# Expert row lists summed from one-hot products on chip instead of read back from HBM, in a decoder-step kernel

## The chip, the cores and the metric

The kernel runs on one core of one Trainium2 chip. The metric is the device time of one launch in microseconds, the median of several runs. The profile is one execution of the same program taken by the hardware profiler; its times count from the start of its span.

## What is computed

One layer of a hybrid decoder over 512 prompt tokens and 8 x 4 sample tokens (544 rows of width 1024, all float32). A token-mixing half (a gated delta rule beside a forgetting attention) is followed by the channel-mixing half, where the change lies:

```python
def _moe(h, w_router, router_bias, w_gate, w_up, w_down, ws_gate, ws_up, ws_down):
    s = jax.nn.sigmoid((x @ w_router).astype(jnp.float32))
    sb = s + router_bias.astype(jnp.float32)
    grp = sb.reshape(n_tok, N_GROUPS, N_EXPERTS // N_GROUPS)
    gscore = jnp.sum(lax.top_k(grp, 2)[0], axis=-1)
    _, gidx = lax.top_k(gscore, TOPK_GROUPS)
    ...
    _, eidx = lax.top_k(jnp.where(emask, sb, -jnp.inf), TOP_K)
    ...
    def expert(acc, xs):
        wg, wu, wd, ge = xs
        y = (jax.nn.silu(x @ wg) * (x @ wu)) @ wd
        return acc + ge[:, None] * y.astype(jnp.float32), None
    ...
    shared = (jax.nn.silu(x @ ws_gate) * (x @ ws_up)) @ ws_down
```

Each token goes to 8 of 64 experts (inner width 256), and all tokens to one shared expert of the same width.

## The kernel before

The program is a series of phases. The last one, from about 715 us on, holds the output projection, the layer norm, the router, the shared expert, the routed experts and the final sum. Tokens lie in five tiles: 0 to 3 of 128 rows, tile 4 of the 32 sample rows.
The router's part, per tile t: TensorE transposes the normed rows (`h2_transposes`) and makes the `logits`; ScalarE takes the sigmoid; VectorE picks eight experts (`choose`, 22 short instructions in a chain); TensorE counts, by a product with a triangular matrix, how many earlier tokens chose each expert (`place`); VectorE makes from it the address 768 x expert + place of each of the token's eight entries (`address`). POOL then writes the token's entry numbers to these addresses of a list in HBM, one indirect DMA for each of the eight columns (`enter` on POOL, 34 in all). After the last tile `totals`, `counts`, `rank_experts` and `sort` order the experts by the number of their tokens. The order goes to HBM (`order_row`), where SP reads it to load expert weights by rank (`load_by_rank`).

The routed experts run as 46 units, a list fixed when the program is built. A unit serves 128 rows of one expert, or of two whose lists are short. POOL reads the lists back in rank order (`ranked`, one gather), VectorE doubles and quadruples their heads (`twice`, `quad`), TensorE transposes them (`unit_rows`), and VectorE makes row numbers of them for the gathers and scatters of all units (`unit_indices`).

Then comes the loop over units. TensorE, unit u: transposes of unit u-1's hidden rows (`hiddenT`), transposes of unit u+1's tokens (`xT`), gate/up product of u (`gate_up_of`), down product of u-1 (`down_of`). Weights sit in a ring of four gate/up slots and five down slots, 3 MB an expert; the load of expert n waits for the last unit that used its slot. POOL gathers tokens three units ahead and scatters each unit's rows.

The shared expert fills gaps: `up(t)` ahead of the loop between the router's products, then `shared_hidden`, `down(t)`, `shared_fold`. Before the change `down` of tiles 0, 1, 2 stands ahead of the loop and those of tiles 3 and 4 stand in it as `shared_step`s (`SHARED_BESIDE`).

## Time and profile before

| what | value |
| --- | --- |
| median of 3 runs | 1521.06 us |
| lowest, highest | 1520.38, 1523.2 us |
| profiled execution, its time | 1513.65 us |
| its span | 1511.8 us |
| mean granted clock of TensorE | 0.964 |
| TensorE (PE) busy | 1383.9 us, 92% |
| VectorE (DVE) busy | 562.8 us, 37% |
| ScalarE (ACT) busy | 291.6 us, 19% |
| GpSimd (POOL) busy | 316.0 us, 21% |
| moved by DMA | 358.50 MB |

Busy time counts an engine's own work, not its waits. A granted clock of 1.00 is full speed. DMA share is the mean busy share of the core's 16 DMA engines.

### The profile page before, as it was taken

Reading aid. Unit: us, or ns where it says so; the run is one execution under the profiler, and the core shown is the slowest. Engines: PE = TensorE matmul, PEld = TensorE weight load, DVE = VectorE, ACT = ScalarE, POOL = GpSimd, SP = SyncE. Lnnn points to the kernel's source line nnn. Section 1 sums busy time; section 2 is a strip of 40 time slices with the busy share of each in tenths; the row PEclk is TensorE's granted clock in tenths of the full one; section 3 lists DMA queues with packets and bytes.
Section 4 is the critical chain, followed back from the end, with each engine's and each line's share of the span. In section 5 each row is a group of like instructions: output and inputs, shape, how many; then the busy total and the mean of one; then the engine's idle time right before and its main releaser. Section 6 shows DMA issues by size and latency. Waiting matters only on the chain. (4 is left out here: it accounts for less than half of the span.)

```text
span 1511.8 us, 21981 instructions
## 1 busy us (share of the span) xinstructions
PE 1383.9 (92%) x8512; PEld 790.9 (52%) x8512; DVE 562.8 (37%) x1292; ACT 291.6 (19%) x674; POOL 316.0 (21%) x334
## 2 busy tenths in 40 slices
PE   5999999999969999899998799998999999999966
PEld 3776777764657776776454334443344333434322
DVE  1101455453633654445886243211111111111138
ACT  1002233453223222111111011111011111101021
POOL 6000000000069994000054111111112111111100
PEclk9999999999989999989999899999999999999988
DMA  9510410123464443685006789999999999999585
GB/s 338 173 56 8 143 58 1 56 85 112 135 185 138 140 138 94 216 289 185 29 29 180 265 362 396 408 415 417 420 401 401 412 419 389 416 412 420 204 315 226
DMA packets 106804, 358.50 MB, mean 237 GB/s; under 512 B 28837, under 2 KB 31013, under 8 KB 80581
## 3 DMA queue, kind: packets, MB, share of 16 engines
q1 hardware_dynamic: 81288, 301.98, 52.0%
q0 software_dynamic: 15968, 40.61, 7.3%
q10 hardware_dynamic: 9446, 14.51, 2.8%
q8 instruction: 68, 1.11, 0.3%
q14 instruction: 34, 0.28, 0.1%
HBM read 331.49 MB, written 38.15 MB: 245 GB/s over the span
## 5 line engine op out<-in xcount | busy, mean ns | idle before, releaser
L2134 PE MATMUL bank<-arena 128*32 128x512 f32 (+2 forms) x1536 | 335.1, 618 | 19.6 <-DMA arena<-in_w_up 17.7
L2134 PEld LDWEIGHTS bank<-arena 128*32 128x32 f32 (+2 forms) x1536 | 121.1, 138 | 201.3 <-issue 198.5
L2142 PE MATMUL bank<-arena 128*32 128x512 f32 (+2 forms) x768 | 168.6, 598 | 0.7 <-DVE arena L2915 0.7
L2121 POOL DMA_INDIRECT expert_rows<-arena x46 | 46.4, 1008 | 485.4 <-PE bank L2127 418.6
L2909 DVE TENSOR_TENSOR arena<-arena,bank 128x256 f32<-128x256 f32 x46 | 19.4, 421 | 320.7 <-ACT arena L2556 320.7
L1210 PE MATMUL bank<-arena 128*128 128x272 f32 x512 | 128.7, 404 | 1.9 <-ACT arena L1247 1.6
L438 PE MATMUL bank<-arena 128*128 128x272 f32 x480 | 113.8, 400 | 2.8 <-PEq L132 1.9
L2142 PEld LDWEIGHTS bank<-arena 128*32 128x32 f32 (+2 forms) x768 | 55.0, 134 | 110.3 <-issue 109.4
L1210 PEld LDWEIGHTS bank<-arena 128*128 128x128 f32 x512 | 95.8, 193 | 28.0 <-issue 7.1
L438 PEld LDWEIGHTS bank<-arena 128*128 128x128 f32 x480 | 92.9, 194 | 23.1 <-issue 2.8
L668 PE MATMUL bank<-arena 128*128 128x272 f32 x384 | 100.3, 405 | 0.0
L455 PE MATMUL bank<-arena 128*128 128x512 f32 (+3 forms) x320 | 91.9, 448 | 0.5 <-DVE arena L2691 0.5
L2556 ACT ACTIVATE arena<-bank 128x256 f32<-128x256 f32 x46 | 17.7, 384 | 344.3 <-PE bank L2134 344.3
L2921 DVE COPY arena<-bank 128x512 f32<-128x512 f32 x46 | 31.8, 692 | 126.9 <-PE bank L2142 126.9
L668 PEld LDWEIGHTS bank<-arena 128*128 128x128 f32 x384 | 70.4, 193 | 13.9 <-issue 1.5
L455 PEld LDWEIGHTS bank<-arena 128*128 128x128 f32 (+1 forms) x320 | 50.3, 199 | 40.8 <-issue 38.6
L2618 POOL DMA_INDIRECT expert_lists<-arena x34 | 38.0, 1117 | 128.1 <-DVE arena L2749 118.7
L2562 ACT COPY arena<-bank 128x512 f32<-128x512 f32 x46 | 27.0, 587 | 152.4 <-PE bank L2142 152.4
L2117 POOL DMA_INDIRECT arena<-h_rows,arena x46 | 46.3, 1007 | 35.1 <-issue 20.8
L1727 POOL MEMSET arena<- 64x128 f32 x2 | 0.4, 198 | 253.1 <-POOLq L1252 253.0
L2127 PE MATMUL bank<-arena 128*128 128x128 f32 x368 | 48.6, 276 | 4.7 <-DVE arena L2771 3.6
L2127 PEld LDWEIGHTS bank<-arena 128*128 128x128 f32 x368 | 42.6, 143 | 5.8 <-DVE arena L2771 3.9
(485 smaller groups left out, 1788.9 us busy)
## 6 DMA issues: line engine op xcount, KB each, us to landing
arena<-in_w_gate SPq DMA_DIRECT2D x64, 1024.0 KB
arena<-in_w_up SPq DMA_DIRECT2D x64, 1024.0 KB
arena<-in_w_down SPq DMA_DIRECT2D x64, 1024.0 KB, 15.3
arena<-in_w_ada SPq DMA_DIRECT2D x12, 2048.0 KB, 9.4
arena<-in_w_in SPq DMA_DIRECT2D x11, 2048.0 KB, 9.9
arena<-expert_rows SPq DMA_DIRECT2D x8, 2048.0 KB, 25.5
gate_logits<-arena ACTq DMA_DIRECT2D x16, 272.0 KB, 3.8
arena<-gate_logits SPq DMA_DIRECT2D x8, 544.0 KB, 5.0
```

The costliest lines, as they stand in the source:

```text
L438: mm = nc.tensor.matmul(pair[i][:, 0:HALF], w[:, k, m * P:(m + 1) * P], rhs[:, k, i * HALF:(i + 1) * HALF], start=k == 0, stop=k == kt - 1)
L455: mm = nc.tensor.matmul(out, lhs[:, k, t * P:t * P + n], w[:, k, cols], start=k == 0, stop=k == kt - 1)
L668: mm = nc.tensor.matmul(out[:, 0:HALF], w[:, k, (m % 4) * P:(m % 4 + 1) * P], hT[:, k, half * HALF:(half + 1) * HALF], start=k == 0, stop= ...
L1210: mm = nc.tensor.matmul(out[:, 0:HALF], w[:, k, m * P:(m + 1) * P], hT[:, k, half * HALF:(half + 1) * HALF], start=k == 0, stop=k == KD - 1)
L2117: return nc.gpsimd.indirect_dma_start(out=into, out_offset=None, in_=h2_d, in_offset=bass.IndirectOffsetOnAxis(ap=rows, axis=0), bounds_ch ...
L2121: return nc.gpsimd.indirect_dma_start(out=y_d, out_offset=bass.IndirectOffsetOnAxis(ap=rows, axis=0), in_=of, in_offset=None, bounds_check ...
L2127: mm = nc.tensor.transpose(bank[half][:, k * P:(k + 1) * P], of[:, kk * P:(kk + 1) * P], ident)
L2134: mm = nc.tensor.matmul(out[rows].rearrange("p (a n) -> p a n", a=2), x[:, k, rows], gate_up_slot(n)[:, :, k, :], start=k == 0, stop=k == ...
L2142: mm = nc.tensor.matmul(out[rows, :], h[:, k, rows], down_slot(n)[:, k, 512 * half:512 * half + 512], start=k == 0, stop=k == 1)
L2562: nc.scalar.copy(Yb[u % RY][:, 0:512], bank[5][:, :]).then_inc(y_a.sem, 1)
L2618: scat.inc(nc.gpsimd.indirect_dma_start(out=list_rows, out_offset=bass.IndirectOffsetOnAxis(ap=adi[:, t, k:k + 1], axis=0), in_=tokval[:, ...
L2921: nc.vector.tensor_copy(Yb[u % RY][:, 512:D], bank[6][:, :]).then_inc(y_v.sem, 1)
```

## The change

The list entries of a tile become two sets of one-hot rows: `ent_e` marks, for each of the eight columns, the token's expert (64 wide, scaled by the entry's number less a constant), and `ent_p` marks the place in that expert's list (192 wide). TensorE multiplies them and sums over all columns and tiles in one PSUM bank (`enter` on TensorE, 34 products), which leaves the first 192 places of every list on chip. One-hot rows are made on POOL for tiles 0, 1, 2 and on VectorE for tiles 3 and 4. `unit_rows` becomes four products with the sorting one-hot `hot`, so that it sorts and transposes at once. POOL still scatters the entries to HBM, where only overflow beyond the fixed units is read: tile 0 as before, tiles 1 to 4 after the first three token gathers. `down` of tile 2 moves into the loop, so that three tiles stand there (`BESIDE`), with another order in each unit. The order of TensorE's list around `enter` is new, VectorE's behind `order_and_excess` too. The load of the first `w_down` waits for the last list product, because one of the `ent_p` tiles lies in its slot.

```diff
@@ -2042,6 +2044,8 @@
         for name, dst, tick in (("w_gate", both[:, 0], gu), ("w_up", both[:, 1], gu), ("w_down", down_slot(n), dn)):
             if name == "w_gate" and n >= RG:
                 sp.wait_ge(gu_mm.sem, LAST_UNIT[n - RG] + 1)
+            if name == "w_down" and dn is dl[0] and n == 0:
+                sp.wait_ge(list_mm.sem, 2 * PT + 1)
             if name == "w_down" and n >= RD:
                 sp.wait_ge(d_mm.sem, LAST_UNIT[n - RD] + 1)
...
 
             def unit_rows():
                 pe.wait_ge(dup_done.sem, 1)
-                nc.tensor.transpose(bank[5][:, 0:E], ranked[:, 0:P], ident[0:E, 0:E])
-                nc.tensor.transpose(bank[5][:, E:2 * E], twice.rearrange("p a n -> p (a n)"), ident[0:E, 0:E])
-                nc.tensor.transpose(bank[5][:, 2 * E:3 * E], ranked[:, P:2 * P], ident[0:E, 0:E])
-                unit_mm.inc(nc.tensor.transpose(bank[5][:, 3 * E:4 * E], quad.rearrange("p a n -> p (a n)"), ident[0:E, 0:E]))
+                nc.tensor.matmul(bank[7][:, 0:E], lists[:, 0:P], hot, start=True, stop=True)
+                nc.tensor.matmul(bank[7][:, E:2 * E], twice.rearrange("p a n -> p (a n)"), hot, start=True, stop=True)
+                nc.tensor.matmul(bank[7][0:ROWS - P, 2 * E:3 * E], lists[:, P:ROWS], hot, start=True, stop=True)
+                unit_mm.inc(nc.tensor.matmul(bank[7][:, 3 * E:4 * E], quad.rearrange("p a n -> p (a n)"), hot, start=True, stop=True))
+
...
+                n = 4 if t < PT else 2
+                pe.wait_ge(ent_made.sem, 2 * t + half + 1) if t < 3 else pe.wait_ge(ent_late.sem, 2 * t + half - 5)
+                for k in range(n):
+                    mm = nc.tensor.matmul(bank[7][E * (k % 2):E * (k % 2) + E, 0:ROWS], ent_e[:, 4 * half + k, :], ent_p[half][:, k, :],
+                                          start=t == 0 and half == 0 and k < 2, stop=t == PT and k >= n - 2)
+                list_mm.inc(mm)
 
             for depth in (range(KD - 1), range(KD - 1, KD)):
                 if depth[0]:
...
@@ -2332,30 +2348,39 @@
                 if t < 2:
                     place(t)
             h2_transposes(3)
-            up(0, 0, 1)
+            up(0, 0, 3)
             place(2)
             logits(3)
-            up(0, 1, KD)
+            up(0, 3, KD)
             h2_transposes(4)
             up(1, 0, 1)
+            enter(0, 0)
+            enter(0, 1)
             logits(4)
-            up(1, 1, 3)
+            up(1, 1, 4)
             place(3)
-            up(1, 3, 6)
+            enter(1, 0)
+            enter(1, 1)
+            up(1, 4, 6)
             place(4)
             up(1, 6, KD)
             counts()
             up(2, 0, 2)
             sort()
-            up(2, 2, KD)
+            enter(2, 0)
+            enter(2, 1)
+            up(2, 2, 5)
             overflow_sums()
-            down(0)
+            enter(3, 0)
+            enter(3, 1)
+            enter(4, 0)
+            up(2, 5, KD)
+            unit_rows()
             up(3)
             table()
             up(4)
-            unit_rows()
+            down(0)
             down(1)
-            down(2)
 
             def shared_step(kind, t):
 
...
-            pe.wait_ge(s_fold.sem, 3)
+            pe.wait_ge(s_fold.sem, 1)
             for u in range(NU):
                 if u:
                     hiddenT(u - 1)
                 if u + 1 < NU:
                     xT(u + 1)
+                if 1 <= u <= len(BESIDE):
+                    shared_step("high", BESIDE[u - 1])
                 gate_up_of(u)
-                if u in SHARED_BESIDE:
-                    shared_step(*SHARED_BESIDE[u][0])
+                if u < len(BESIDE):
+                    shared_step("hiddenT", BESIDE[u])
                 if u:
                     down_of(u - 1)
-                if u in SHARED_BESIDE:
-                    shared_step(*SHARED_BESIDE[u][1])
+                if u < len(BESIDE):
+                    shared_step("low", BESIDE[u])
             hiddenT(NU - 1)
             down_of(NU - 1)
             pe.wait_ge(y_a.sem, NU)
...
-            pool.wait_ge(side_store.sem, 16)
-            for t in range(NT):
+            step = chained(pool, gch)
+            TT, TS = nc.gpsimd.tensor_tensor, nc.gpsimd.tensor_scalar
+
+            def enter_tile(t):
                 pool.wait_ge(addr_done.sem, t + 1)
                 for k in range(TOPK if t < PT else 2):
                     enter(t, k)
-            pool.wait_ge(order_done.sem, 2)
-            pool.wait_ge(x1_done.sem, NT)
-            pool.wait_ge(scat.sem, scat.n)
-            lists_in.inc(nc.gpsimd.indirect_dma_start(out=ranked, out_offset=None, in_=list_d,
-                                                      in_offset=bass.IndirectOffsetOnAxis(ap=order_i.bitcast(U32), axis=0)), 16)
+
+            def one_hots(t):
+                pool.wait_ge(addr_done.sem, t + 1)
+                if t:
+                    pool.wait_ge(list_mm.sem, 2 * t)
+                step(TS(expert_of, a8[:, t, :], 1.0 / LC, -0.5 - 0.5 / LC, ALU.mult, ALU.add))
+                step(TS(expert_of, expert_of, 12582912.0, None, ALU.add))
+                step(TS(expert_of, expert_of, 12582912.0, None, ALU.subtract))
+                step(TS(expert_of, expert_of, float(LC), None, ALU.mult))
+                step(TT(place_of, a8[:, t, :], expert_of, ALU.subtract))
+                for k in range(TOPK):
+                    step(TS(ent_e[:, k, :], key[:, t, :], a8[:, t, k:k + 1], short_val[:, t, k:k + 1], ALU.is_equal, ALU.mult))
+                for k in range(TOPK):
+                    ins = TS(ent_p[k // 4][:, k % 4, :], place1, place_of[:, k:k + 1], None, ALU.is_equal)
+                    ent_made.inc(ins) if k % 4 == 3 else step(ins)
+
+            step(pool.iota(place1, pattern=[[1, ROWS]], base=1, channel_multiplier=0, allow_small_or_imprecise_dtypes=True))
+            pool.wait_ge(tokval_made.sem, 3)
+            step(TS(short_val, tokval, -float(FILL), None, ALU.add))
+            pool.wait_ge(side_store.sem, 16)
+            enter_tile(0)
+            pool.wait_ge(wo_mm.sem, 2 * NT)
+            one_hots(0)
+            one_hots(1)
+            one_hots(2)
...
@@ -2645,6 +2690,8 @@
             pool.wait_ge(su_mm.sem, NT)
             for u in range(RX - 1):
                 gather(u)
+            for t in range(1, NT):
+                enter_tile(t)
             for u in range(NU):
                 if u + RX - 1 < NU:
...
@@ -2750,8 +2797,9 @@
                 else:
                     for q in range(4):
                         rows = slice(QUAD * q, QUAD * q + QUAD)
-                        ins = TS(adi[rows, t, 0:2], a8[rows, t, 2 * q:2 * q + 2], -1.0, None, ALU.add)
-                        done(addr_done, ins) if q == 3 else vch.inc(ins)
+                        ins = nc.vector.tensor_copy(a8s[rows], a8[rows, t, 2 * q:2 * q + 2])
+                        step(ins) if q == 3 else vch.inc(ins)
+                    done(addr_done, TS(adi[:, t, 0:2], a8s, -1.0, None, ALU.add))
...
+            def one_hots(t):
+                n = TOPK if t < PT else 2
+                found, where, to = (a8[:, t, :] if t < PT else a8s), place_of[:, 0:n], expert_of[:, 0:n]
+                over_e, over_p = [P, n, E], [P, min(n, 4), ROWS]
+                dve.wait_ge(list_mm.sem, 2 * t)
+                step(TS(to, found, 1.0 / LC, -0.5 - 0.5 / LC, ALU.mult, ALU.add))
+                step(TS(to, to, 12582912.0, None, ALU.add))
+                step(TS(to, to, 12582912.0, None, ALU.subtract))
+                step(STT(where, to, -float(LC), found, ALU.mult, ALU.add))
+                step(TT(ent_e[:, 0:n], key[:, t, :].unsqueeze(1).to_broadcast(over_e), found.unsqueeze(2).to_broadcast(over_e), ALU.is_equal))
+                step(TT(ent_e[:, 0:n], ent_e[:, 0:n], short_val[:, t, 0:n].unsqueeze(2).to_broadcast(over_e), ALU.mult))
+                for half in range(max(1, n // 4)):
+                    here = where[:, 4 * half:4 * half + min(n, 4)].unsqueeze(2).to_broadcast(over_p)
+                    done(ent_late, TT(ent_p[half][:, 0:min(n, 4)], place1.unsqueeze(1).to_broadcast(over_p), here, ALU.is_equal))
+
+            def lists_out():
+                dve.wait_ge(list_mm.sem, 2 * PT + 1)
+                step(nc.vector.tensor_copy(lists, bank[7][:, 0:ROWS]))
+                step(nc.vector.tensor_copy(quad, bank[7][:, 0:QUAD].unsqueeze(1).to_broadcast([P, 4, QUAD])))
+                done(dup_done, nc.vector.tensor_copy(twice, bank[7][:, 0:64].unsqueeze(1).to_broadcast([P, 2, 64])))
+
...
+                for rows, a, b, c in ((slice(0, P), 0, WIDE, 0), (last, THREE, WIDE, 3 * E + SMALL), (low, WIDE, PAIRED, 2 * E),
+                                      (high, WIDE, PAIRED, E + WIDE), (low, PAIRED, NU, E + PAIRED), (high, PAIRED, NU, E + PAIRED + 6)):
+                    step(TS(units_f[rows, a:b], got[rows, c:c + b - a], float(FILL), None, ALU.add))
                 done(unit_done, row_indices(step, units_f, floor_f, to_rows, from_rows))
...
@@ -2874,23 +2936,24 @@
             totals()
             rank_experts()
             order_and_excess()
+            one_hots(3)
+            one_hots(4)
             shared_hidden(0)
             shared_hidden(1)
+            lists_out()
+            overflow_rows()
+            unit_indices()
+            shared_hidden(2)
             residual(3)
+            overflow_table()
             residual(4)
-            shared_hidden(2)
-            overflow_rows()
+            shared_hidden(3)
+            shared_hidden(4)
             shared_fold(0)
-            shared_hidden(3)
-            overflow_table()
-            shared_hidden(4)
-            unit_indices()
...
+            xT_high(0)
             shared_fold(1)
-            xT_high(0)
-            shared_fold(2)
             for u in range(NU):
                 if u:
                     hiddenT(u - 1)
                 if u + 1 < NU:
                     xT_high(u + 1)
+                if 1 <= u <= len(BESIDE):
+                    fold_beside(1, BESIDE[u - 1])
                 hidden(u)
-                if u in SHARED_BESIDE:
-                    fold_beside(*SHARED_BESIDE[u][0])
                 if u:
                     y_high(u - 1)
-                if u in SHARED_BESIDE:
-                    fold_beside(*SHARED_BESIDE[u][1])
+                if u < len(BESIDE):
+                    fold_beside(0, BESIDE[u])
```

## Rows read from the trace of the kernel before

**Rows 1.** Table of stretches: from:to, length, busy us (instructions) by engine, clock, DMA share, GB/s.
```profile
777.40:857.00 79.60, 63.25 (x224) 32.65 (x222) 47.05 (x163) 10.86 (x20) 33.79 (x32) 0.87 0.62 210
...
869.90:883.90 14.00, 14.00 (x81) 5.28 (x81) 4.51 (x9) 1.51 (x5) 0.00 (x0) 1.00 0.79 317
...
957.00:1441.00 484.00, 459.31 (x2301) 190.32 (x2299) 82.02 (x154) 59.66 (x115) 75.42 (x75) 0.98 0.96 391
```

**Rows 2.** Timeline of PE, 794 to 899 us: start, us, line, shapes, count, idle before.
```profile
794.74 0.68 PE L2228 MATMUL bank<-arena 32*128 32x32 f32 x8 [0.91 <-DVE arena L2707]
...
796.33 2.00 PE L455 MATMUL bank<-arena 128*128 128x64 f32 x16
...
803.05 0.43 PE L2244 MATMUL bank<-arena 32*128 32x64 f32 x2
...
818.46 6.10 PE L2288 MATMUL bank<-arena 128*128 128x512 f32 x8 [3.81 <-ACT arena L2514]
824.39 7.03 PE L2262 MATMUL bank<-arena 128*128 128x512 f32 x16
...
831.51 3.65 PE L2260 MATMUL bank<-arena 128*32 128x256 f32 x32
836.54 0.27 PE L2311 MATMUL bank<-arena 64*128 64x64 f32 x1 [1.39 <-DVE arena L2839]
...
839.55 5.37 PE L2288 MATMUL bank<-arena 128*128 128x512 f32 x8 [2.12 <-DVE arena L2061]
...
845.60 3.70 PE L2288 MATMUL bank<-arena 128*128 128x512 f32 x8 [0.46 <-ACT arena L2514]
...
856.98 8.98 PE L2134 MATMUL bank<-arena 128*32 128x512 f32 x64
...
898.50 1.04 PE L2127 MATMUL bank<-arena 128*128 128x128 f32 x8
```

**Rows 3.** Timeline of POOL, 814 to 841 us.
```profile
814.27 0.95 POOL L2618 DMA_INDIRECT expert_lists<-arena  x1 [0.30 <-issue]
815.53 0.96 POOL L2618 DMA_INDIRECT expert_lists<-arena  x1 [0.30 <-issue]
824.98 0.95 POOL L2628 DMA_INDIRECT arena<-expert_lists,arena  x1 [8.49 <-DMA expert_lists<-arena]
840.27 1.04 POOL L2117 DMA_INDIRECT arena<-h_rows,arena  x1 [14.34 <-DVE arena L2061]
```

**Rows 4.** Timeline of DVE, of choose, the order's copy, the last of unit_indices.
```profile
766.42 0.41 DVE L2739 TENSOR_SCALAR arena<-arena 128x64 f32<-128x64 f32 x1
...
808.45 0.21 DVE L2791 CAST arena<-bank 1x64 int32<-1x64 f32 x1 [0.59 <-PE bank L2297]
...
839.21 0.19 DVE L2061 CAST arena<-arena 128x46 uint32<-128x46 f32 x1
```

**Rows 5.** Table of stretches, while POOL scatters entries and little else moves.
```profile
786.00:792.00 6.00, 6.00 (x13) 2.68 (x13) 5.12 (x9) 1.71 (x3) 4.78 (x5) 0.73 0.02 0
```

**Rows 6.** The page's costliest groups: busy us, mean ns, then idle before.
```profile
L438 PE MATMUL bank<-arena 128*128 128x272 f32 x480 | 113.8, 400 | 2.8 <-PEq L132 1.9
```

**Rows 7.** Groups of POOL by form: busy us, mean ns, then idle before.
```profile
L1766 POOL TENSOR_SCALAR arena<-arena 128x2048 f32<-128x2048 f32 x4 | 21.8, 5442 | 0.4
...
L1762 POOL TENSOR_SCALAR arena<-arena 128x32 f32<-128x32 f32 x4 | 1.5, 367 | 0.4
...
L1746 POOL COPY arena<-arena 64x128 f32<-64x128 f32 x2 | 0.6, 288 | 2.5 <-DMA arena<-sample_gates 2.5
...
L1770 POOL COPY arena<-arena 128x32 f32<-128x32 f32 x1 | 0.2, 210 | 0.1
```

**Rows 8.** Timelines of DVE, POOL and DVE again, earlier in the kernel.
```profile
501.27 2.53 DVE L1553 TENSOR_TENSOR arena<-arena 128x256 f32<-128x256 f32 x1
...
501.18 2.35 POOL L1756 TENSOR_TENSOR arena<-arena 128x1024 f32<-128x1024 f32 x1
...
623.59 0.43 DVE L1553 TENSOR_TENSOR arena<-arena 128x256 f32<-128x256 f32 x1
```

More of the change, by code:

```diff
@@ L1878, in build @@
     gsc, rank8, v8 = (scratch(NT, 8) for i in range(3))
-    adi, base = scratch(NT, 8, dt=U32), scratch(E)
+    base = scratch(E)
     m1s, m2s, ent = scratch(OVER, p=E), scratch(OVER, p=E), scratch(2, p=E)
-    nsort, keyp, rank = scratch(2, p=E), scratch(1, p=E), scratch(1, p=E)
+    nsort, keyp, rank = scratch(2, p=E), scratch(1), scratch(1)
     by_rank, excess, over, sums = scratch(2, p=E), scratch(1, p=E), scratch(1, p=E), scratch(2, p=E)
-    order_i = scratch(1, p=E, dt=I32)
     tab_f, tab_i, count_i = scratch(2, p=OVER), scratch(2, p=OVER, dt=I32), scratch(1, p=E, dt=I32)
-    keyf, cmp_, hot = (at(X0 + 15616 + E * i, E, p=E) for i in range(3))
+    keyf, cmp_, hot = (at(X0 + 15616 + E * i, E) for i in range(3))
     h2_d = nc.dram_tensor("h2_rows", (TOK, D), F32).ap()
@@ L2061, in row_indices @@
         return nc.vector.tensor_copy(to_rows, slots_f)
-    ranked = at(X0 + 12800, LC, p=E)
-    twice, quad = at(X0 + 13568, 2, 64, p=E), at(X0 + 13696, 4, QUAD, p=E)
+    twice, quad, lists = at(X0 + 13568, 2, 64), at(X0 + 13696, 4, QUAD), at(X0 + 13824, ROWS)
+    ent_e, ent_p = at(T2 + 1024, TOPK, E), (at(T1 + 1024, 4, ROWS), at(DN_SLOT[0], 4, ROWS))
+    place1 = at(T1 + 1024 + 4 * ROWS, ROWS)
+    short_val, place_of = at(T1 + 1024 + 5 * ROWS, NT, TOPK), at(T1 + 1064 + 5 * ROWS, TOPK)
+    expert_of, a8s = at(T1 + 1072 + 5 * ROWS, TOPK), at(T1 + 1080 + 5 * ROWS, 2)
+    assert T1 + 1082 + 5 * ROWS <= T1 + 2048 and DN_SLOT[0] + 4 * ROWS <= T1 + 6912 and T2 + 1536 <= WS0
     units_f, floor_f = at(T2, NU), at(T2 + NU, NU)
@@ L2298, in sort @@
-                sort_mm.inc(nc.tensor.matmul(bank[7][0:E, 260:262], hot, nsort, start=True, stop=True))
+                sort_mm.inc(nc.tensor.matmul(bank[4][0:1, 320:384], nsort[:, 0:1], hot[0:E], start=True, stop=True))
+                sort_mm.inc(nc.tensor.matmul(bank[5][0:E, 260:262], hot[0:E], nsort, start=True, stop=True))
             def overflow_sums():
                 pe.wait_ge(over_done.sem, 1)
-                nc.tensor.matmul(bank[7][0:E, 264:265], cumU[0:E, 0:E], over, start=True, stop=True)
@@ L2303, in overflow_sums @@
-                cum_mm.inc(nc.tensor.matmul(bank[7][0:E, 265:266], ones[0:E, 0:E], over, start=True, stop=True))
+                nc.tensor.matmul(bank[5][0:E, 264:265], cumU[0:E, 0:E], over, start=True, stop=True)
+                cum_mm.inc(nc.tensor.matmul(bank[5][0:E, 265:266], ones[0:E, 0:E], over, start=True, stop=True))
             def table():
                 pe.wait_ge(row_done.sem, 1)
-                tab_mm.inc(nc.tensor.matmul(bank[7][0:OVER, 268:270], m1s, ent, start=True, stop=True))
+                tab_mm.inc(nc.tensor.matmul(bank[5][0:OVER, 268:270], m1s, ent, start=True, stop=True))
@@ L2512, in shared_hiddenT @@
                     act.wait_ge(sd_mm.sem, t)
-                src = bank[4 if t < 3 else 7]
+                src = bank[4 if t < 2 else 7]
                 sT_sb.inc(nc.scalar.copy(shT[:, :, 0:n], src[:, 0:2 * n].rearrange("p (k n) -> p k n", k=2)))
@@ L2839, in unit_indices @@
-                done(dup_done, nc.vector.tensor_copy(twice, ranked[:, 0:64].unsqueeze(1).to_broadcast([E, 2, 64])))
                 dve.wait_ge(unit_mm.sem, 1)
-                got = bank[5]
+                got = bank[7]
                 low, high, last = slice(0, 64), slice(64, P), slice(96, P)
-                step(nc.vector.tensor_copy(units_f[:, 0:WIDE], got[:, 0:WIDE]))
-                step(nc.vector.tensor_copy(units_f[last, THREE:WIDE], got[last, 3 * E + SMALL:4 * E]))
-                step(nc.vector.tensor_copy(units_f[low, WIDE:PAIRED], got[low, 2 * E:2 * E + HEAVY]))
```

71 lines of the change are left out of this document (31 added, 40 removed).

## The prediction, made before the changed kernel was run

> **What bounds the kernel now.** I read the page's slices first (where TensorE has holes), then the timelines of the four engines between 763 and 857 us, which is where the diff works, then the table of stretches for the loop over the 46 units behind it. The chain that ended last reaches back only to 1438 us, so it says nothing of this stage.
>
> The loop is closed from both sides [rows 1]: in its second unit, from 869.9 to 883.9 us, TensorE is busy all the time with DMA at 0.79, and from 957 to 1441 us TensorE is busy 459 of 484 us with DMA at 0.96. The reader should see that the loop can't be compressed: it ends a fixed time after it begins. So I ask when the first gate/up product can run. Before, that is at 857.0 us [rows 2].
>
> What leads up to it is a relay. The router's choices become list entries, which POOL scatters to HBM with 34 indirect DMAs, the last at 815.5 us; it waits 8.5 us for them to land, reads the lists back at 825.0 us [rows 3], and the row numbers are ready at 839.4 us [rows 4]. Beside that relay TensorE is not idle: from 777.4 to 857 us it is busy 63.25 of 79.6 us [rows 1]. Only the holes, 16.35 us, can be won there, and of those that the timeline names (0.9, 3.8, 1.4 and 2.1 us [rows 2]) the read-back of the lists explains the last two.
>
> **The change, part by part.**
>
> *Removed.* The wait of 8.5 us, the gather of the lists (825.0 to about 834 us) and one of three shared down products ahead of the loop. Gain on the path: at most the holes above and the product's 0.4 + 3.7 us [rows 2].
>
> *Moved.* 26 of the 34 scatters now stand behind the first three token gathers: 26 x 1.26 us [rows 3] = 33 us of POOL, in front of the gather for unit 3 and the scatter of unit 0. Before, the gathers begin at 840.3 and unit 3's rows are transposed at 898.5 [rows 2, 3], 58 us later; behind the change that gather is issued some 37 us after the first and lands about 10 us later, as the first did (840.3 to 850.4). Hidden by about 11 us; if that cover went, unit 3 would be late. The scatters themselves keep the DMA engines 2% busy [rows 5], 26 of them under 1 us.
>
> *Added on TensorE.* 34 one-hot products with 192 columns. Nearest row: 272 columns, 113.8 us for 480 instructions, 0.237 us each [rows 6]; two instructions are one f32 product, so 192/272 x 0.47 = 0.335 us, and 34 of them 11.4 us. Bounds: 8.5 us (64 columns, 2.00 us for eight products [rows 2]) and 16.1 us (as 272 columns).
>
> *Added on POOL, for tiles 0, 1 and 2.* Each tile is a chain of 21 elementwise instructions, each waiting for the last: 5 of 8 columns, 8 of 64, 8 of 192. The trace has `TENSOR_SCALAR` with a per-partition scalar at 32 columns, 0.366 us, and at 2048 columns, 5.44 us [rows 7], so 2.5 ns a column upon 0.28 us: 0.445 us at 64 and 0.77 us at 192 columns. With 0.25 us for a small one and gaps of 0.085 us: 1.2 + 3.6 + 6.1 + 1.8 = 12.7 us a tile, 9.3 us until its first half is ready. Lower bound from the copy rows, 0.21 us at 32 and 0.29 us at 128 columns [rows 7]: about 7.6 us a tile. I take 12.7, since it is the same operation.
>
> The Trainium skill ("GPSIMD Engine Reference", 4.1 Engine selection) calls one-input elementwise work on GpSimd roughly line-rate; the `TENSOR_SCALAR` row disagrees, the copy rows nearly agree. By that rule a tile would cost about the lower bound and the sum below would be that of the rival "quick POOL".
>
> *What VectorE pays.* With POOL busy, VectorE's two-operand instruction on 256 columns took 2.53 us; it ended at 503.80, 0.27 us behind the POOL instruction that had begun just before it. The same line with POOL idle takes 0.43 [rows 8]. `choose` has 10 instructions of the exposed kinds (7 two-operand ones in SBUF, 3 `TENSOR_SCALAR`; the second kind I count by the 0.41 us that L2739 once took instead of 0.19 [rows 4]). Each waits for what is left of a POOL instruction, about 0.4 us: +4 us a `choose`. POOL waits for them in turn: about +3 us a tile.
>
> The Trainium skill ("SBUF — State Buffer", Who interferes with whom) says the same of these two engines: whichever issues first holds the shared pair for its whole instruction.
>
> *The relay, step by step.* Serialization is the point: `one_hots(t)` on POOL waits until the products of tile t-1 are done, and TensorE meets `enter(t)` in its fixed order, with `place`, `counts` and `sort` queued behind.
> - POOL's tile 0 starts when out_rows(4) is done, 777.5, and ends near 795 (12.7 + 4.5 for VectorE's holds).
> - `choose(2)` +4, the layer norm of tile 4 a little: its h2 is ready at 799.4 instead of 794.7.
> - TensorE: transposes 0.7, up(1,0,1) 1.0, `enter(0)` 2.7: done 803.8.
> - POOL's tile 1: 803.9 + 12.7 + 3.5 = 820.1; `enter(1)` done 821.4. Meanwhile TensorE has only logits(4) 2.0, up 3.0, place(3) 0.6 to do: it stands from 809.4 to 815.5 and again 3 us.
> - up 2.0, `place(4)`: 824, against 803.05 before. Then address(4), totals, counts, ranks, sort: 5.6 us before (803.05 [rows 2] to 808.66 [rows 4]), 8.8 with POOL's tile 2 beside it: the sorted order at 832.6, 24 us later, and with it the first expert weights.
> - POOL's tile 2: 821.5 + 12.7 + 3.8 = 838; `enter(2)` done 839.3.
> - VectorE's tile 3: four small ones 0.8, two of 512 columns and two of 768, which from 0.43 us at 256 [rows 8] are at most 0.86 and 1.3 each; with 0.7 and 1.0, since part of the 0.43 is fixed, 4.2 us: 843.5. `enter(3)` 845.4, tile 4 and its entries 848.0, up(2,5,8) 3.0 beside `lists_out`, `unit_rows` 852.5.
> - up(3) 7.0, up(4) 3.7 (as before [rows 2]): 863.3; POOL's gathers wait for it too: 863.4 instead of 840.3.
> - down(0), down(1) 5.3 each: 873.9; two sets of transposes, first gate/up product 876.5.
>
> So the loop begins 19.5 us later. SP is held as well: `w_down` of load 0 waits for the last list product (848), loads 1 and 2 queue behind it, and 7 MB from 848 at about 400 GB/s are there by 866, before 876.5: no cost, as long as TensorE is that late. In the loop stand 4.1 us more of shared products (a third tile), in units 0 to 3, where TensorE has no hole but DMA has some left (0.79 [rows 1]): I count 2 us of them. Behind the loop nothing changes.
>
> **Sum.** 19.5 + 2 = 21.5 us. The profiled execution took 1513.65 us (span 1511.8), so 1535 for the like; the runs' median is 1521.06, 7.4 us above it, and with the same shift I get 1542.5; I give 1541, since not every exposed instruction will meet POOL in mid-flight.
>
> **Rivals.**
> - *POOL slow, but no blocking of VectorE.* Same relay with 12.7 us a tile and nothing else: h2 of tile 4 at 794.7, `enter(0)` 799.1, tile 1 811.9, `place(4)` 815.7, order 820.7, tile 2 826, `unit_rows` 840.5, gathers 851.3, first product 864.3: +7.3 + 2 = +9.5: 1530. Against it: the 2.53 us.
> - *Quick POOL*, 7.6 us a tile, with blocking: `enter(1)` 812.9, tile 2 822.5, `unit_rows` 838.2, gathers 849, first product 862: +5 + 2 = +7: 1528.
> - *Products ready in time (faster).* If a tile on POOL took under about 5 us, each `enter` would find its one-hots made. Then up(4) ends at 835.2 - 4.1 (holes) - 6.6 (down(0) moved behind) + 11.4 + 1.5 = 837.4; gathers land about 848; down(0), down(1) fill the gap; first product 851.2, 5.8 us earlier, of which the third tile in the loop takes back about 2: -4, 1517. It decides only below 5 us; the cheapest rows give 7.6.
> - *No net change*: the same with half of that eaten by colder clock or the late SP queue: 1521.
> - *Late scatters bite*: if POOL's issue in the loop were slowed by a third or more, unit 3 waits: up to +8 upon the forecast, 1550.
>
> **How the numbers follow.** Forecast 0.50, no blocking 0.18, quick POOL 0.12, late scatters 0.05, faster 0.07, same 0.08. A measurement of this kernel can tell about 0.2%, 3 us. Faster 0.07, same 0.08, slower 0.85. The forecast's own range, from the bounds of the products (-3, +5) and of blocking, is 1534 to 1549; leaving out faster, most of same and the top gives 1524 to 1550.
>
> **What would show it.** Right: POOL's 128x192 instructions at 0.7 us or more; TensorE waiting on POOL ahead of `enter(1)` and `enter(2)` for 15 us together; the store of the sorted order some 20 us later; the first token gather near 863. Wrong: those instructions near 0.35 us, `choose(2)` still 3.9 us long, or a first gate/up product before 857. A wrong slope at 192 columns moves all of it: each 0.1 us there is 0.8 us a tile.

## The result, and the profile of the changed kernel

The changed kernel takes 1560.59 us (median; 1553.21 to 1563.27), the kernel before, run beside it on the same chip, 1522.88: ratio 1.0227, interval 1.019 to 1.0264. It is slower by about 2.3%. The prediction had the direction, but at 1541 us, with a range that ended at 1550, it was too low.

The profiled execution took 1553.21 us (span 1551.1), 39.3 us more of span than the one of before. The first view is TensorE's timeline, the part that answers to [rows 2]: start, us, line, shapes, count, idle before and what ended it.

```profile
791.40 1.06 PE L2237 MATMUL bank<-arena 32*128 32x32 f32 x8 [5.37 <-DVE arena L2754]
...
797.16 2.54 PE L456 MATMUL bank<-arena 128*128 128x64 f32 x16
...
808.00 1.55 PE L2328 MATMUL bank<-arena 128*64 128x192 f32 x8 [5.29 <-POOL arena L2663]
811.32 1.54 PE L2328 MATMUL bank<-arena 128*64 128x192 f32 x8 [1.76 <-POOL arena L2663]
...
815.98 0.43 PE L2253 MATMUL bank<-arena 32*128 32x64 f32 x2
...
826.88 1.55 PE L2328 MATMUL bank<-arena 128*64 128x192 f32 x8 [2.44 <-POOL arena L2663]
...
837.18 0.55 PE L2328 MATMUL bank<-arena 128*64 128x192 f32 x4 [2.19 <-DVE arena L2896]
...
867.82 5.55 PE L2142 MATMUL bank<-arena 128*32 128x512 f32 x39
...
875.92 1.61 PE L2142 MATMUL bank<-arena 128*32 128x512 f32 x2 [1.49 <-issue]
...
880.87 1.01 PE L2142 MATMUL bank<-arena 128*32 128x512 f32 x1 [0.40 <-issue]
...
894.20 1.87 PE L2142 MATMUL bank<-arena 128*32 128x512 f32 x2 [1.79 <-issue]
```

Two things are to be seen. In the upper half the relay of the prediction is there: TensorE waits for GpSimd's one-hots ahead of the list products, and `place(4)`, the line of 2 with 32x64, comes late. In the lower half is something that no step of the prediction has. Unit 0's gate/up product starts at 867.82, and after 39 matmul instructions TensorE begins them one or two at a time. The product is over at 898.7, 30.8 us after its start; before, it took 9.0 [rows 2]. The engine waits for nothing that the profile names ("issue").

The second view is the table of stretches, with the columns of [rows 1]: the stretch from the first late entry DMA until the slow part begins, the slow part, the second unit, and the loop.

```profile
857.20:872.40 15.20, 10.94 (x60) 4.83 (x63) 6.42 (x10) 1.37 (x3) 11.83 (x12) 0.89 0.82 328
872.40:897.00 24.60, 14.59 (x27) 1.93 (x19) 0.00 (x0) 0.00 (x0) 15.66 (x16) 0.59 0.13 35
904.97:921.30 16.33, 15.92 (x85) 6.22 (x85) 5.55 (x13) 1.93 (x4) 2.33 (x2) 1.00 0.74 286
957.00:1441.00 484.00, 461.03 (x2314) 192.40 (x2312) 90.36 (x206) 60.40 (x116) 77.88 (x77) 0.98 1.00 410
```

In 24.6 us TensorE begins 27 matmul instructions, while VectorE and ScalarE begin none and the DMA engines are at 0.13. The granted clock is 0.59 there, but it isn't the cause: a matmul takes 1 us at it, and each group of one or two starts 1.4 to 2.8 us behind the last, with an idle gap between. GpSimd is the one engine that works, and its timeline says on what (it answers to [rows 3]; the last lines of two groups of one-hots stand ahead).

```profile
783.12 10.59 POOL L2663 TENSOR_SCALAR arena<-arena 128x192 f32<-128x192 f32 x8
...
798.98 5.54 POOL L2661 TENSOR_SCALAR arena<-arena 128x64 f32<-128x64 f32 x8
804.62 6.64 POOL L2663 TENSOR_SCALAR arena<-arena 128x192 f32<-128x192 f32 x8
...
853.12 1.14 POOL L2125 DMA_INDIRECT arena<-h_rows,arena  x1 [26.30 <-PE bank L2269]
...
857.18 1.03 POOL L2641 DMA_INDIRECT expert_lists<-arena  x1 [0.30 <-issue]
...
889.29 0.97 POOL L2641 DMA_INDIRECT expert_lists<-arena  x1 [0.30 <-issue]
890.57 1.05 POOL L2125 DMA_INDIRECT arena<-h_rows,arena  x1 [0.30 <-issue]
891.92 1.01 POOL L2125 DMA_INDIRECT arena<-h_rows,arena  x1 [0.30 <-issue]
```

The 26 late entry DMAs and the two gathers behind them run from 857.2 to 892.9. TensorE is back at full pace at 896.3.

**Where the 39.3 us are.** From TensorE's marks in both traces: start of the stage to the transposes of tile 4, -3.3 (791.40 against 794.74); from there to the first gate/up product, +14.2 (76.42 against 62.24); unit 0's product, +21.9; the rest of the way to unit 1, +2.4; units 1 to 3, +2.8; the loop behind that, +1.8; behind the loop, -0.4 (39.4 by rounding). The gate/up products of units 3 and 4 start at 937.42 and 949.07, against 899.47 and 911.13.

**How good the trace of before is.** There is one, and its execution was 7.4 us quicker than the median. The kernels of experiments 2, 5 and 6 below run the instructions of before up to the first gather (some tiles lie elsewhere in memory). From the transposes of tile 0 to the first gate/up product their traces have 132.6, 131.2 and 131.1 us, the trace of before 126.5, the changed kernel 140.5. So measured against those three, the part ahead of the loop costs 8 to 9 us and not 14. In two of them (experiments 2 and 5) ScalarE takes up the transposes of tile 4 some 6 us after their start instead of 0.5, while GpSimd issues 16 entries in a row, and TensorE waits for it. From experiment 2:

```profile
798.45 0.68 PE L2229 MATMUL bank<-arena 32*128 32x32 f32 x8 [0.98 <-issue]
...
805.64 3.68 PE L455 MATMUL bank<-arena 128*128 128x64 f32 x16 [5.46 <-ACT arena L2495]
```

How often the kernel before does this is not shown.

### The profile page after: what moved, and what is told of

Its sections match the earlier page's. It is cut to its first block and busy times, and to the rows that moved or that the text cites. A ratio compares the mean times of both kernels' runs of the same rounds, so it can differ in the third digit from the quotient of the medians.

```text
span 1551.1 us, 22214 instructions
## 1 busy us (share of the span) xinstructions
PE 1400.2 (90%) x8586; PEld 793.8 (51%) x8586; DVE 569.6 (37%) x1308; ACT 291.7 (19%) x674; POOL 352.2 (23%) x399
## 5 line engine op out<-in xcount | busy, mean ns | idle before, releaser
L2142 PE MATMUL bank<-arena 128*32 128x512 f32 (+2 forms) x1536 | 345.5, 612 | 33.0 <-DMA arena<-in_w_up 22.1
L2150 PE MATMUL bank<-arena 128*32 128x512 f32 (+2 forms) x768 | 168.6, 598 | 0.7 <-DVE arena L2978 0.7
L2581 ACT ACTIVATE arena<-bank 128x256 f32<-128x256 f32 x46 | 17.7, 384 | 374.7 <-PE bank L2142 374.7
L669 PEld LDWEIGHTS bank<-arena 128*128 128x128 f32 x384 | 70.1, 193 | 13.9 <-issue 1.7
L456 PEld LDWEIGHTS bank<-arena 128*128 128x128 f32 (+1 forms) x320 | 48.4, 191 | 41.1 <-issue 39.3
L2641 POOL DMA_INDIRECT expert_lists<-arena x34 | 33.3, 981 | 70.7 <-DVE arena L2796 60.6
```

Of the source, the lines that this page charges most:

```text
L456: mm = nc.tensor.matmul(out, lhs[:, k, t * P:t * P + n], w[:, k, cols], start=k == 0, stop=k == kt - 1)
L669: mm = nc.tensor.matmul(out[:, 0:HALF], w[:, k, (m % 4) * P:(m % 4 + 1) * P], hT[:, k, half * HALF:(half + 1) * HALF], start=k == 0, stop= ...
L2142: mm = nc.tensor.matmul(out[rows].rearrange("p (a n) -> p a n", a=2), x[:, k, rows], gate_up_slot(n)[:, :, k, :], start=k == 0, stop=k == ...
L2150: mm = nc.tensor.matmul(out[rows, :], h[:, k, rows], down_slot(n)[:, k, 512 * half:512 * half + 512], start=k == 0, stop=k == 1)
L2641: scat.inc(nc.gpsimd.indirect_dma_start(out=list_rows, out_offset=bass.IndirectOffsetOnAxis(ap=adi[:, t, k:k + 1], axis=0), in_=tokval[:, ...
```

## The experiments

Each was run beside the kernel before; its median there lay between 1514 and 1525 us, so ratios are compared.

**1. Without the late entries.** The rows of tiles 1 to 4 are not entered into the lists in HBM; nothing reads them with this input. SyncE's wait for the entries is lowered to the eight that are left (not shown).

```diff
-            for t in range(1, NT):
-                enter_tile(t)
             for u in range(NU):
```

> The changed kernel without the 26 list-entry DMAs of tiles 1 to 4 that POOL issues after the first three token gathers (their entries are left out of the HBM lists, which only overflow units read). Theory A (these DMAs starve TensorE in unit 0, where the first gate/up product took 30.8 us instead of 9.0): that product is back near 9 us and the kernel is about 22 us faster than the changed one, some 16 us slower than before. Rival B (the slow product comes from something else at the start of the loop, as the cold clock or where an instruction page ends): it stays near 30 us and the time stays near 38 us above before.

Measured: 1535.66 us, ratio 1.009 [1.0059, 1.0122]. The DMAs alone are worth 0.0137 of 1523 us by the ratios, 21 us (the two intervals leave some 7 us either way), and 25 by the medians. Unit 0's product is whole again:

```profile
873.25 9.18 PE L2142 MATMUL bank<-arena 128*32 128x512 f32 x64
```

**2. The kernel before, with 26 late entries.** The same entries are written a second time, behind the first three gathers (values and addresses stay in memory of their own for it).

```diff
             for u in range(RX - 1):
                 gather(u)
+            for t in range(1, NT):
+                for k in range(TOPK if t < PT else 2):
+                    enter(t, k)
```

> The kernel before, with its 34 entries as they were, and 26 of them issued a second time after the first three token gathers (same addresses, same values; two scratch tiles moved so that weights don't overwrite them). Nothing else of the change. Theory A: the first gate/up product goes from 9 to about 30 us and the kernel is some 22 us slower than before. Rival B: the product keeps 9 us; POOL's 33 us are hidden behind units 0 and 1, and the time is within 3 us of before.

Measured: 1551.78 us, ratio 1.0197 [1.0133, 1.0261]; 30 us by the ratio, 27 by the medians. Nothing of the change is in this kernel but the late row of DMAs, and its TensorE timeline has the same stretch:

```profile
866.62 5.45 PE L2135 MATMUL bank<-arena 128*32 128x512 f32 x37
872.42 0.59 PE L2135 MATMUL bank<-arena 128*32 128x512 f32 x1 [0.35 <-issue]
...
892.84 1.01 PE L2135 MATMUL bank<-arena 128*32 128x512 f32 x1 [0.40 <-issue]
894.23 4.37 PE L2135 MATMUL bank<-arena 128*32 128x512 f32 x15 [0.38 <-issue]
```

So it is the DMAs, wherever they came from, and not the one-hots or the lists on chip.

**3. The changed kernel, the entries before the gathers.** `enter_tile(1)` to `(4)` stand right behind `one_hots(2)` on GpSimd.

> The changed kernel with the 26 list-entry DMAs moved ahead of the first token gather, into the 26 us in which POOL waited for the shared up products. They need 33 us, so the gathers start about 7 us later (860 instead of 853). Theory A: no slow product; 22 - 7 = 15 us faster than the changed kernel, about 23 us slower than before. Rival B: the 30 us product stays and the 7 us come on top, about 45 us slower than before.

Measured: 1548.97 us, ratio 1.019 [1.0125, 1.0256]. Unit 0's product takes 7.6 us now; the slow stretch has moved with the DMAs (831.3 to 865.2 us) to the shared up product of tile 4:

```profile
853.01 2.35 PE L2269 MATMUL bank<-arena 128*32 128x256 f32 x18
...
861.67 1.31 PE L2269 MATMUL bank<-arena 128*32 128x256 f32 x2 [2.42 <-issue]
...
868.70 1.87 PE L2269 MATMUL bank<-arena 128*32 128x256 f32 x6 [0.81 <-issue]
```

The slow stretch lasts some 15 us here, from 855.4 on. The gathers wait for that product, so the loop is late instead of slow: the first gate/up product comes 91.0 us after the transposes of tile 4, against 76.5 in experiment 1. Over experiment 1 the entries cost 13 to 15 us here, against 21 to 25 behind the gathers. Theory A's number (23 us above before) is near the 24 by the medians, but by luck: it had expected no slow product at all.

**4. Eight at a time.** One tile's entries behind the scatter of each of four units.

> The changed kernel with one tile's entries (8, 8, 8, 2 DMAs) issued behind each of the scatters of units 3 to 6, when the loop is under way. Theory A: unit 0 is back at 9 us, and the gate/up or down products beside each group of 8 DMAs (10 us of POOL) are slowed, the more so the more instructions they have in a microsecond: units of four 32-row groups most. Rival B: unit 0 stays at 30 us and no product beside the groups is slowed.

Measured: 1551.84 us, of one run. Unit 0 is at 8.0 us, and the unit's product beside the first eight DMAs takes 7.07 us, as without them: TensorE itself isn't slowed by eight in a row, against the expectation. But ScalarE is. Its activation behind that product starts at 958.44, 7.8 us after the product's end (0.1 us in experiment 1), though both semaphores that it waits for had been set, and TensorE waits for it through VectorE:

```profile
958.44 0.38 ACT L2581 ACTIVATE arena<-bank 128x256 f32<-128x256 f32 x1 [14.48 <-DMA gate_logits<-arena]
```
```profile
959.33 0.70 PE L2425 MATMUL bank<-arena 128*128 128x128 f32 x2 [5.03 <-DVE arena L2972]
```

(The DMA that the first line names is of a much earlier phase.) Behind that, TensorE waits 4.47 us for a gather that stood behind eight entries, and 3.38 for expert weights.

**5. Twelve of them.** Kernel of experiment 2 with 12 late entries.

> The kernel before with 12 instead of 26 entry DMAs repeated after the first three gathers (26 of them gave 1551.78 us, plus 27 us, with TensorE slow from about 13 DMAs on until 5 us after the last). If the slow stretch needs a long row of DMAs ahead of it, 12 cost 0 to 3 us: up to 1528 us. If the price is in proportion to their number, plus 12 us: about 1537 us. If the slow stretch only begins when TensorE has used up some 125 instructions after their start, it begins where the 12 end, and costs up to 5 us.

Measured: 1526.72 us, ratio 1.0027 [1.0002, 1.0051]. Unit 0's product takes 11.8 us instead of 9.0, with one gap of 0.81 us by "issue" near 874 us, just behind the last of the DMAs. The price is not in proportion: 3 to 4 us for 12 (0 to 8 by the interval), 27 for 26. Most of it comes with what the row has beyond the first dozen. Whether the onset goes by the number of DMAs or by what TensorE has executed since, as the expectation asks, this run doesn't tell.

**6. Direct DMAs instead.** Kernel before, with 26 direct DMAs of 128 x 4 bytes from SyncE's queue, to a spare tensor, behind the weight loads of unit 3.

```diff
             load_by_rank(sp, 3)
+            for i in range(26):
+                spare_out.inc(sp.dma_start(spare_d[i], tokval[:, 1 + i // TOPK, i % TOPK:i % TOPK + 1]), 16)
```

> The kernel before with 26 direct DMAs of 128 x 4 bytes each, queued by SyncE to a spare tensor behind the weight loads of unit 3, in place of the 26 repeated indirect ones from GpSimd's queue. If small DMAs as such slow TensorE, unit 0's gate/up product takes 25 to 31 us here too, and the time is near 1550 us. If it is the indirect DMAs out of GpSimd's queue, the product takes 9 us and the time is within 3 us of before, plus what load 4 loses behind 26 issues.

Measured: 1528.51 us, ratio 1.0035 [1.0013, 1.0057]. SyncE's queue is busy with them for 28.7 us, nearly as long as the 33 us of GpSimd's, and TensorE's product beside them is as before:

```profile
845.59 28.71 SPq L2182 DMA_DIRECT2D spare_rows<-arena  x26
```

```profile
863.94 9.08 PE L2137 MATMUL bank<-arena 128*32 128x512 f32 x64
```

So small transfers as such are not it; a long row of indirect DMAs out of GpSimd's queue is. Whether it is that they are indirect or that they are GpSimd's, this run doesn't separate.

**7. The order of the relay.** From here on the other part, +14.2. The late entries are left out, and TensorE meets `place(4)`, `counts` and `sort` ahead of the products of tile 1 (and `up(2, 2, 5)` and `overflow_sums` ahead of those of tile 2, not shown).

```diff
             place(3)
-            enter(1, 0)
-            enter(1, 1)
             up(1, 4, 6)
             place(4)
             up(1, 6, KD)
             counts()
             up(2, 0, 2)
             sort()
+            enter(1, 0)
+            enter(1, 1)
```

> The changed kernel without its 26 late entry DMAs, and on TensorE place(3), place(4), counts and sort are moved ahead of the one-hot products of tile 1 (before: 1535.66 us without the move). The prediction's step was that the order is late because TensorE, which waits for GpSimd's one-hots ahead of place(3) and place(4), passes the delay on to everything behind it. If that alone sets the relay, the cast of the order comes some 13 us earlier, and so do the gathers and the first gate/up product: near 1522 us. Rival, which I now hold likelier: the order comes 13 us earlier, but the gathers do not, since GpSimd's own chain of three tiles (776 to 827 us of the changed kernel) with two more tiles on VectorE behind it ends where it ended: 1533 to 1537 us, gathers within 2 us of where they stood from the stage's first entry DMA.

Measured: 1537.45 us, ratio 1.0092 [1.0064, 1.012]; without the move it was 1.009. The order does come early, and it buys nothing:

```profile
809.86 0.43 PE L2253 MATMUL bank<-arena 32*128 32x64 f32 x2
...
828.46 1.55 PE L2328 MATMUL bank<-arena 128*64 128x192 f32 x8 [7.45 <-POOL arena L2663]
...
841.74 0.91 PE L2328 MATMUL bank<-arena 128*64 128x192 f32 x4 [2.19 <-DVE arena L2894]
```

The wait that stood ahead of `place(4)` now stands ahead of `enter(2)`. From the transposes of tile 4, `place(4)` is 13.0 us away (24.6 in the changed kernel), the last list product 44.9 (45.8), the first gate/up product 78.0 (76.4). GpSimd's chain of three tiles, with VectorE's two behind it, sets the end, not the order in which TensorE passes it on.

**8. One tile less on GpSimd.** As 7, with the one-hots of tile 2 on VectorE, shared up products in TensorE's gaps and `logits(4)` ahead of the products of tile 0 (the last two not shown).

```diff
             one_hots(0)
             one_hots(1)
-            one_hots(2)
```
```diff
             order_and_excess()
+            shared_hidden(0)
+            shared_hidden(1)
+            one_hots(2)
             one_hots(3)
             one_hots(4)
-            shared_hidden(0)
-            shared_hidden(1)
```

> The changed kernel without its late entry DMAs, with the TensorE order of the last run, the shared up products of tiles 2 and 3 put in the gaps, and the one-hots of tile 2 made by VectorE instead of GpSimd (GpSimd keeps tiles 0 and 1). If GpSimd's chain of three tiles sets the end of the lists, this takes the lists to about 828 us (three tiles of 4.5, 4.5 and 2 us on VectorE from 812 us) and then the last shared up product sets the gathers, near 836 us instead of 853: 1517 to 1522 us. If something else of the relay binds (TensorE's own work of 34 one-hot products), it stays above 1528 us.

Measured: 1523.12 us, ratio 1.0005 [0.9985, 1.0024]: 13 us less than 7. TensorE is busy nearly without a gap up to the gathers, and the first product comes 63.2 us after the transposes of tile 4 (62.2 before, 76.4 in the changed kernel):

```profile
837.75 0.55 PE L2328 MATMUL bank<-arena 128*64 128x192 f32 x4 [0.28 <-DVE arena L2895]
...
862.24 7.71 PE L2142 MATMUL bank<-arena 128*32 128x512 f32 x64
```

The order on TensorE and the place of one tile together give back the relay; the share of each is not separated. The time is just above the 1517 to 1522 us expected. From the transposes of tile 0 the first product comes after 127.1 us, 4 to 5 us less than in the traces of experiments 2, 5 and 6, so the idea does gain ahead of the loop. But from there to unit 4's product it takes 58.1 us, against 54.2 in the trace of before and in that of experiment 6: the third shared product takes the gain back.

**9 and 10. The entries in pairs.** Two behind each scatter of 13 units, in the kernel of experiment 1 and in that of 8. All of the work is done in both.

```diff
                 if u:
                     scatter(u - 1)
+                for t, k in late_entries[2 * (u - 4):2 * (u - 3)] if u >= 4 else ():
+                    enter(t, k)
```

> The changed kernel with its 26 late entry DMAs taken from behind the first gathers and put two at a time behind the scatters of 13 units, from the fourth on: all of its work is done. If only a long row of indirect DMAs slows TensorE, pairs cost nothing there, and each gather comes at most 2.6 us later, which a gather that is issued units ahead can bear: 1534 to 1538 us, no part of a unit slower than without them. If each such DMA has a price wherever it stands (26 in a row cost 25 us), it is above 1545 us.

> The version with the one-hots of tile 2 on VectorE and TensorE's order changed (1523.12 us, 1.0005 of before, without late entries), now with the 26 late entries in pairs behind the scatters of 13 units, so that all of the work is done: 1521 to 1526 us, within 0.3% of before. If the pairs have a price, 1530 us or more.

Measured: 1552.58 us, ratio 1.0174 [1.0141, 1.0207], and 1538.38 us, ratio 1.0085 [1.0057, 1.0113]. Both expectations missed and the rivals with a price held, by the same sum: 0.0084 and 0.0080 of 1523 us, 12 to 13 us for 26 DMAs (each with some 6 to 7 us either way; that they agree so well is partly chance). No product is slow by its instructions this time; the units wait for expert weights:

```profile
996.93 8.77 PE L2142 MATMUL bank<-arena 128*32 128x512 f32 x64 [4.47 <-DMA arena<-in_w_up]
...
1027.62 9.24 PE L2142 MATMUL bank<-arena 128*64 128x512 f32 x32 [5.28 <-DMA arena<-in_w_up]
```

The table of stretches, first of the kernel without the entries (experiment 1), then with pairs (9):

```profile
940.00:1100.00 160.00, 154.48 (x792) 64.38 (x793) 35.22 (x103) 20.53 (x40) 26.23 (x26) 0.99 1.01 416
```

```profile
940.00:1100.00 160.00, 143.02 (x711) 58.91 (x713) 33.09 (x99) 18.70 (x36) 48.05 (x48) 0.95 1.00 379
```

DMA is full in both. With 24 entries in the stretch it moves 60.7 MB instead of 66.5, and 5.8 MB at 416 GB/s are 14 us: by this estimate 0.6 us of the whole weight stream for each DMA of 0.5 KB.

**11. The entries only when they are read.** Kernel of 8, with the 26 entries inside the branch that runs when an expert overflows (the one reader of the lists in HBM), and the overflow table made earlier on VectorE. Nothing is left out; the branch is not taken with this input.

```diff
-            late_units(pool, "pool", late)
+            late_units(pool, "pool", late, lambda: [enter(t, k) for t in range(1, NT) for k in range(TOPK if t < PT else 2)])
```

> The version with the one-hots of tile 2 on VectorE and TensorE's order changed (1523.12 us, 1.0005 of before, where the late entries were left out), with the 26 entries moved into the branch that runs only when some expert has more rows than its unit holds (nothing else reads them), so that nothing is left out for any input; and the overflow rows and table are made earlier on VectorE, so that ScalarE's copy for the first shared down product doesn't wait for them (3.03 us idle of TensorE there). Expected: the copy wait falls to about 0.5 us, the first gate/up product comes some 2 us earlier, 1519 to 1523 us, ratio 0.997 to 1.001. Rival: the three weight loads that wait for the list products set the first product through the gathers that land beside them (2.68 us idle before the second transposes), and the gain is eaten there: the same as without it, 1523 us.

Measured: 1522.28 us, ratio 1.0051 [1.0026, 1.0077]. The wait for ScalarE's copy fell from 3.03 to 0.46 us as expected:

```profile
848.03 3.70 PE L2295 MATMUL bank<-arena 128*128 128x512 f32 x8 [0.46 <-ACT arena L2542]
```

But the first product is 62.1 us behind the transposes of tile 4, only 1.1 us better than 8 (TensorE then waits 1.85 and 2.67 us for the gathers), and the ratio missed the expected 0.997 to 1.001. The 1522.28 us lie in the expected range only because this chip is quicker: the kernel before had 1514.13 there. The rival, that the gain is eaten by the gathers, held. It is the best whole version of the idea that I ran. It does not beat the old kernel.

## Why the prediction was wrong, step by step

**The failed step** is in "Moved": "The scatters themselves keep the DMA engines 2% busy, 26 of them under 1 us", with the row of 26 held to cost only what stands behind it on POOL. I asked who waits for GpSimd's queue, and found 11 us of cover; I did not ask what the row does to an engine that waits for nothing in it. With the row in flight TensorE begins 27 matmul instructions in 24.6 us, though it waits for nothing that the profile names: 21 to 30 us (experiments 1 and 2). The rival "late scatters bite" had the right culprit and the wrong mechanism, a late gather for unit 3, and 0.05. The row that I used [rows 5] could not show it: five such DMAs ran there in 6 us, and TensorE was busy throughout. The 2% was also the wrong measure: beside a full stream such a DMA costs 0.5 to 0.6 us, not 0.04 (experiments 9 and 10).

**The relay** was right in kind and too dear. In the clock of the trace of before (3.3 us added to the changed kernel's times): `place(4)` at 819.3 for 824; order at 824.9 for 832.6; gathers at 856.4 for 863.4; first product 871.2 for 876.5, so +14.2 for +19.5. Measured against the traces of experiments 2, 5 and 6 it is 8 to 9 us, which is further from the forecast.

- *POOL's chain*, 12.7 us a tile: 13.9 and 13.8 for tiles 1 and 2. 0.83 us at 192 columns and 0.69 at 64, gap included, where I had 0.855 and 0.53. The size at 192 columns was right. The 64-column instruction was dearer; it has two operations where the other has one, so the pair gives no slope. By the Trainium skill ("GPSIMD Engine Reference", 4.1 Engine selection), which calls such work roughly line-rate, the tile would have taken about 7.6 at the pace of the copy rows [rows 7]; the trace disagrees.
- *Blocking of VectorE*, +4 us a `choose`: wrong, and in its direction. `choose(4)` took 4.1 us (3.9 before) in the middle of GpSimd's tile, and the layer norm of tile 4 has the durations of before. GpSimd paid: its eight 192-column instructions took 10.59 us instead of 6.64 beside VectorE's layer norm of tile 4. That gave tile 0 its 17.7 us (12.7 + 4.5 predicted, for the wrong reason). The shared port of the Trainium skill ("SBUF — State Buffer", Who interferes with whom) is there in tile 0, but not as a toll on each short VectorE instruction, as I had used it from one row of 2.53 us [rows 8].
- *List products*, 11.4 us for 34 (68 instructions): 10.4 us, the sum of their seven lines, right.
- *The rival "POOL slow, but no blocking"* came nearer than the forecast up to `unit_rows`: its `place(4)` at 815.7, `unit_rows` at 840.5 and first product at 864.3 stand against 819.3, 843.7 and 871.2. (The forecast had 824, 852.5 and 876.5.) At the first product the forecast is the nearer, 5.3 us off for 6.9: since its blocking was wrong, that is luck. The rival was given 0.18.
- *What sets the end*: I had written that TensorE's fixed order passes the delay on. Experiment 7 refutes that as the cause of the end (`place(4)` and the sort came 11 to 12 us earlier, the loop did not). The chain of tiles does: TensorE waits 7.45 us for GpSimd's tile 2 there, and experiment 8, which shortens the chain and fills gaps at once, has the loop back.

**The third shared product**: 2 us predicted; the units 0 to 3 without unit 0's slow stretch are 5.2 us longer, and the rest of the loop, +1.8, pays nothing back.

**Products ready in time**, the rival on the other side, needed a tile under 5 us; with one tile moved to VectorE its kernel is experiment 8, and it gives no change, not 4 us of gain.

Sum of the forecast: 19.5 + 2 = 21.5. Measured in the profiles: 14.2 + 5.2 + 21.9, less 3.3 ahead of the change and plus 1.4 behind it, 39.4 (39.3 unrounded). Without the missing term the forecast would have been too high, not too low: experiment 1 is at 1.009, 14 us. So the direction was right by the forecast's own terms, and the miss is the one term that it held at nothing.

## What to carry to other kernels

A row of indirect DMAs that is moved out of the way of one queue is not free because nobody waits for it: ask what else runs beside it. Here 26 in a row cost 13 to 30 us, twelve 3 to 4, and eight already held ScalarE once for 7.8 us. Beside a stream that fills the DMA engines each has a price of its own, 0.5 to 0.6 us, even in pairs. Work that only a rare branch reads can be done in that branch. And when a wait is removed from a fixed order of instructions, look where the same wait stands next before counting it. A single trace of the kernel before is a thin base where its parts vary by 5 us.

## What the runs showed of the hardware that was not expected

TensorE can fall idle for microseconds in the middle of a product, with no wait that the profile names. In the changed kernel and in experiments 2 and 3 the pace fell to one or two matmul instructions in 1.4 to 2.8 us after 12 to 19 entry DMAs had been issued back to back, 1.3 us apart, and recovered 4 to 5 us after the start of GpSimd's last indirect DMA. The entries that the kernel before has had all along can do it too: in the kernel of experiment 6, 16 of them stand in a row from 780.6 to 802 us, and TensorE is idle for 6.85 us of that,

```profile
801.57 1.06 PE L2234 MATMUL bank<-arena 32*128 32x32 f32 x8 [6.85 <-issue]
```

which in the trace of before did not happen at that place (0.91 us, for VectorE [rows 2]), though 16 in a row stand there too, from 778.0 to 800.5 us. Nor is TensorE alone held: ScalarE was late by 5 to 8 us beside rows of 16 or 8 in experiments 2, 5 and 4, as said above. From the first late DMA to the onset TensorE had begun 123 instructions in the changed kernel and 129 in that of experiment 2 (matmuls and weight loads), 177 in that of experiment 3. Direct DMAs from SyncE, over 28.7 us, did nothing of the kind. In the changed kernel the DMA engines fetched one page of instructions just as it began, 870 to 872 us, and it took a large share of that time (window of the DMA queues; the page at 914 us behind it has 3.0%):

```profile
q8 instruction: 1, 0.02, 10.7%
```

The Trainium skill ("Runtime: NRT & Kernel Launch", Instruction fetch mechanics) calls the cost of such a page mostly hidden, and no run here shows otherwise. A large share is no sign of the slow stretch: in experiment 6 a page took 12.1% of 876 to 878 us, with TensorE's product beside it at its usual 7.09 us, and in experiment 3 the last page ahead of the slow stretch, at 848 us, took 3.0%. What holds the engines stays open: no run separates the fetch of instructions from other things that GpSimd's descriptor work could hold up.

The second: once the weight stream fills the DMA engines, an indirect DMA of 128 pieces of 4 bytes costs 0.5 to 0.6 us of it (experiments 9 and 10), as much as 0.24 MB of weights.
